# Order and counts changed in a two-layer hybrid decoder step: loads, waits and small tasks around a stream of attention units

## The chip, the core and the metric
The kernel runs on one core of a Trainium2 chip. The metric is the device time of one execution in microseconds, the median of several. The core's engines are TensorE (PE), VectorE (DVE), ScalarE (ACT), GpSimd (POOL) and SyncE (SP), whose queue here issues most of the DMA transfers.

## The reference, cut to what matters
Two layers run one after the other over 1088 rows: a prompt of 1024 tokens, and 8 requests of 8 new tokens each with 2048 cached positions. All numbers are float32.

```python
z = rmsnorm(x, norm1_g) @ w_in                 # 1024 -> 2448, feeds four mixers of 256 channels
o_a = fox attention      # 4 heads, scores + cumulative log forget gates, causal softmax
o_b = silu(layernorm(conv31(ga * sigmoid(gb)) + conv_b))            # 31 taps, per channel
o_c = g0 * compressed + g1 * selected + g2 * windowed attention     # NSA, 4 heads, one kv head
o_d = u * (tril(gmlp_ws) @ layernorm(v) + gmlp_bs)                  # chunks of 128 positions
h = x + concat(rmsnorm(o_i) * gnorm_g[i]) @ w_out
y = h + relu(rmsnorm(h, norm2_g) @ w_ff1)**2 @ w_ff2                # 1024 -> 4096 -> 1024
```
The requests' attention reads paged caches: 16 pages of 128 rows each for a request, of keys and values for fox (o_a) and of four 64-wide rows for NSA (o_c). Besides y, the new keys, values, gates and states are outputs.

## The kernel before, in words
One program per engine is written out by hand, and semaphores order them: `wait_ge(S[name], n)` holds an engine's queue until the count is there, and everything behind it in that queue waits too. A hardware loop runs the body once for each layer.

**Start of a layer.** SyncE issues the layer's small vectors ("gains"), then the token projection's weights into `Wt` in five loads (L656 to L658, counted by `w_tok`). Then come three waits (the residual stored, the normalised rows made, the first squares made) and `xt_free` is raised (L663). `xt_free` tells that the memory of the residual may be overwritten: VectorE waits for it before the taps of the convolution (L1918), GpSimd before its first two loads of raw cache pieces (L2632, two of 16 pieces). Behind it SyncE loads the mixing weights of the gMLP: `WMr` whole in one load (L664), and `WM8r`, an 8x8 corner of the four groups repeated over 8 requests by 8 blocks, in 64 loads (L665 to L668). All 65 loads count into `wm_in`, and VectorE waits for 1040 (16 a load) at L1935 before it masks both (L1937, L1938).
TensorE meanwhile forms the gate products of the convolution (L955), then tile 0 of the token projection (L1042); after that tile's second chunk it needs the masked mixing weights (`mixing_T`, L960 to L969). VectorE runs ten taps (L1911), evicts one gate product (L1923), runs twelve taps, evicts the other (L1928), forms the product with ScalarE's sigmoid, and does the masks. After that nine tiles of the token projection follow, with the other taps between.

**The stream.** Then 96 units follow: 4 heads x 8 query blocks x 3 kinds (fox, selected, windowed). In unit u TensorE forms the scores of unit u + 2, transposes the probabilities of unit u four blocks to a bank ("p" groups), multiplies those of unit u - 1 with the values, and works through the unit's extras. VectorE copies its share of the transposes, takes the row maximum of unit u + 2, and does its extras. ScalarE takes the exponentials of unit u + 1 first, then copies and extras. Every bank of transposes goes through two banks in turn (`open_group`, L1083), so TensorE waits for the copy of the group two before.
The extras are a list by unit (`extras_of`): head transposes and compressed attention, and the requests' attention, one request every ten units from unit 9. Of a request, "kt" transposes the keys of the pages (n = 0 to 7 the fox cache; n = 8 to 11 four NSA pages each; n = 12 the window), "ds" forms scores, "pt" and "pv" the values. kt 8 and 9 stand in the request's sixth unit, kt 10 and 11 in its seventh. The request's 16 NSA pages, its window and three small pieces are loaded by SyncE (`sparse_in`, L745 to L755) once "pv" of the request before is out, and count together into `sl_in`; TensorE waits for 320 per request at n = 8 (L1195).
Other steps in the stream: `gate_totals` (L2126) in unit 4, four scans of the cached gates after a wait for the stores "st0" and their copy; `lateness` (L1275) and `later_sums` (L2137) in unit 7, which make LAT; GpSimd waits for `tot_ready` and then loads the second request's cache, waits for `lat_ready` and then forms its part. `values_out` (L2211) scales the outputs of eight units, and `head_sum` (L2233) adds the three kinds of a head; both stood at the end of units 9, 17, 25, ... behind the extras (L2469 to L2472). `group_sum` (L1693) on ScalarE squares and sums finished outputs, three a unit from unit 84 on, behind the unit's extras (L1740). LAST is 88; unit 89 has "ms", unit 90 has "ee", "gc" and "hs", where "hs" on ScalarE (L1682) waits for the head's last sum from VectorE (`last_head_sum`, L2240).
After the stream the output projection and the two feed-forward products follow, each as three bf16 products (L922 and L1389), the weights streamed through two buffers.

## Time and profile before
| | |
|---|---|
| median of 3 runs | 3395.81 us (3395.05 to 3407.77) |
| the profiled execution | 3396.99 us |
| its span, first to last instruction | 3394.9 us |
| mean granted TensorE clock | 0.984 |
| PE busy | 3261.6 us, 96%, 22642 matmuls |
| DVE busy | 1455.1 us, 43% |
| ACT busy | 1009.0 us, 30% |
| POOL busy | 232.0 us, 7% |
| DMA | 312.51 MB, mean 92 GB/s |
| chain that ended last | PE 86%, DVE 4%, SPq 4%, ACT 3% |
| costliest line | L922, 10080 matmuls, 1549.1 us |

Times in the rows are microseconds from the span's start. A timeline row gives start, length, engine, line, operation, output and input, and the count of instructions merged in it; in brackets stands the idle time of the engine ahead of it, with what ended it. SPq is SyncE's queue of DMA issues; an issue is not the transfer. The granted clock is 1.00 at 2.4 GHz and 0.50 at 1.2 GHz, so a value between is a mix of the two. The first layer runs from about 20 to 1706 us, its stream from about 413 to 901.

### The profile page before, as it was taken

What the parts mean: (1) busy time and instruction counts of PE and PEld (TensorE: products, weight loads), DVE (VectorE), ACT (ScalarE), POOL (GpSimd) and SP (SyncE); (2) the same over time, 40 slices, a digit from 0 to 9 for tenths busy, and PEclk for the clock granted to TensorE, in tenths of its full rate; (3) what the DMA queues carried; (4) which work ended last, traced back from release to release, by engine and by line L of the source; (5) the groups of instructions that cost most, each with busy time, mean ns of one, the idle gap of its engine ahead of it and who ended that gap; (6) DMA issues with size and microseconds to landing.
All of it is one profiled execution on the core that took longest, in us unless ns stands there. A gap on an engine that the chain in (4) does not pass through costs nothing.

```text
span 3394.9 us, 55958 instructions
## 1 busy us (share of the span) xinstructions
PE 3261.6 (96%) x22642; PEld 1888.2 (56%) x22642; DVE 1455.1 (43%) x2795; ACT 1009.0 (30%) x1804; POOL 232.0 (7%) x172
## 2 busy tenths in 40 slices
PE   8899999998899999999999999999989999999998
PEld 5455477776644444444445555767766444444444
DVE  5965653333643311332169566433335432113312
ACT  2113344444423200321102233445453322012211
POOL 1211200000300000000002111000011000000000
PEclk9999999999999999999999999999999999999999
DMA  8423234333311210113153324334322112111322
GB/s 274 118 89 109 83 130 150 127 113 102 106 42 53 68 50 25 43 56 95 51 146 114 107 80 139 136 94 144 132 85 94 44 49 68 44 31 49 83 68 91
DMA packets 375954, 312.51 MB, mean 92 GB/s; under 512 B 121564, under 2 KB 358648, under 8 KB 368376
## 3 DMA queue, kind: packets, MB, share of 16 engines
q1 hardware_dynamic: 367912, 208.59, 21.8%
q0 software_dynamic: 7840, 101.20, 8.0%
q8 instruction: 130, 2.13, 0.3%
q14 instruction: 72, 0.59, 0.1%
HBM read 264.34 MB, written 50.46 MB: 93 GB/s over the span
## 4 chain that ended last, share of the span: by engine, by line
PE 86%; DVE 4%; SPq 4%; ACT 3%; issue 2%; DMA 1%; POOL 0%; POOLq 0%; DVEq 0%; ACTq 0%
PE PS L922 46%; PE PS L1042 13%; PE PS L1310 5%; PE PS L1333 4%; PE PS L1201 2%; PE PS L955 2%; PE PS L1359 2%; PE PS L1017 2%; PE PS L1247 1%; PE PS L1389 1%; SPq L748 1%; DVE arena L1911 1%; SPq L743 1%; PE PS L1003 1%; PE PS L1208 1%
## 5 line engine op out<-in xcount | busy, mean ns | idle before, releaser
L922 PE MATMUL PS<-arena 128*128 128x512 bf16 (+1 forms) x10080 | 1549.1, 317 | 0.0
L922 PEld LDWEIGHTS PS<-arena 128*128 128x128 bf16 x10080 | 753.4, 98 | 794.8
L1042 PE MATMUL PS<-arena 128*128 128x512 f32 (+3 forms) x1152 | 478.0, 570 | 0.0
L1494 ACT ACTIVATE arena<-arena 128x1024 bf16<-128x1024 f32 (+1 forms) x108 | 141.5, 1310 | 1089.3 <-PE PS L922 1076.0
L1042 PEld LDWEIGHTS PS<-arena 128*128 128x128 f32 (+1 forms) x1152 | 208.6, 184 | 236.8 <-issue 203.9
L2506 DVE TENSOR_TENSOR arena<-PS,arena 128x1088 f32<-128x1088 f32 (+1 forms) x48 | 62.0, 1292 | 643.1 <-PE PS L922 632.0
L1310 PE MATMUL PS<-arena 128*128 128x512 f32 (+3 forms) x576 | 232.1, 511 | 10.4 <-ACT arena L1627 5.8
L2532 DVE SCALAR_TENSOR_TENSOR arena<-PS,arena 128x1088 f32<-128x1088 f32 x64 | 82.7, 1292 | 353.1 <-PE PS L922 352.7
L1333 PE MATMUL PS<-arena 128*128 128x64 f32 x1632 | 208.2, 273 | 0.0
L1333 PEld LDWEIGHTS PS<-arena 128*128 128x128 f32 x1632 | 203.0, 196 | 0.0
L1639 ACT ACTIVATE arena<-PS 128x512 f32<-128x512 f32 x208 | 122.1, 596 | 237.2 <-PE PS L1201 236.8
L1561 ACT ACTIVATE arena<-PS,arena 128x512 f32<-128x512 f32 (+6 forms) x144 | 73.9, 581 | 357.9 <-DVEq L2050 227.1
L1911 DVE SCALAR_TENSOR_TENSOR arena<-arena 128x1024 f32<-128x1024 f32 x240 | 175.1, 781 | 2.5
L1877 DVE TENSOR_TENSOR arena<-arena 128x1024 bf16<-128x1024 f32 (+1 forms) x108 | 165.8, 1535 | 20.5 <-ACT arena L1494 20.5
L2195 DVE TENSOR_REDUCE arena<-PS 128x1 f32<-128x1024 f32 (+5 forms) x192 | 137.6, 717 | 65.1 <-PE PS L1313 64.5
L2190 DVE COPY arena<-PS 128x128 f32<-128x128 f32 (+3 forms) x136 | 68.3, 502 | 214.1 <-PE PS L1359 213.6
L1201 PE MATMUL PS<-arena 128*128 128x128 f32 x832 | 130.8, 285 | 25.5 <-DVE arena L2190 8.2
L1627 ACT ACTIVATE arena<-PS,arena 128x1024 f32<-128x1024 f32 (+5 forms) x192 | 135.6, 706 | 31.3 <-DVE arena L2195 31.2
L955 PE MATMUL PS<-arena 128*128 128x512 f32 (+1 forms) x384 | 129.4, 499 | 11.3 <-DVE arena L1886 11.3
L1359 PE MATMUL PS<-arena 128*128 128x128 f32 x816 | 130.6, 284 | 9.3 <-DVE arena L2287 2.6
L1310 PEld LDWEIGHTS PS<-arena 128*128 128x128 f32 x576 | 96.9, 200 | 61.5 <-issue 50.3
L1201 PEld LDWEIGHTS PS<-arena 128*128 128x128 f32 x832 | 96.3, 147 | 43.5 <-DVE arena L2190 10.6
(355 smaller groups left out, 2880.7 us busy)
## 6 DMA issues: line engine op xcount, KB each, us to landing
arena<-in_w_ff SPq DMA_DIRECT2D x64, 512.0 KB, 4.1
arena<-in_w_ff SPq DMA_DIRECT2D x32, 1024.0 KB, 5.7
arena<-in_cache_nsa_kv SPq DMA_DIRECT2D x256, 64.0 KB
x_s<-arena SPq DMA_DIRECT2D x24, 544.0 KB, 3.5
arena<-in_w_in SPq DMA_DIRECT2D x4, 2048.0 KB
arena<-in_w_out SPq DMA_DIRECT2D x16, 512.0 KB, 4.0
arena<-x_s SPq DMA_DIRECT2D x2, 3264.0 KB, 10.4
arena<-in_w_in SPq DMA_DIRECT2D x12, 512.0 KB, 6.7
```

The costliest lines, as they stand in the source:

```text
L922: last = mm(PS[:, 1536 * k + a:1536 * k + a + wd], ww[:, c, :], xx[:, c, a:a + wd], start=c == 0 and n == 0, stop=c == blocks - 1 and n == 2)
L955: last = mm(PS[:, 1536 * s + a:1536 * s + a + n], Wg[:, k, (2 * s + f) * P:(2 * s + f + 1) * P], XNT[:, k, a:a + n], start=k == 0, stop=k ...
L1042: last = mm(PS[0:r, c * 512:c * 512 + b - a], XNT[:, j, t * P:t * P + r], Wt[:, j, a:b], start=j == 0, stop=j == KD - 1)
L1201: last = tr(out[:, j * P:(j + 1) * P], src, ident)
L1310: last = mm(PS[:, at:at + len(part) * P], q[:, i * P:(i + 1) * P], kt[:, part[0] * P:(part[-1] + 1) * P], start=True, stop=not masks)
L1333: last = mm(PS[:, at:at + HD], PTR[u % 2][:, n * P:(n + 1) * P], v, start=n == 0, stop=n == len(js) - 1)
L1359: last = tr(out[:, (j - a) * P:(j - a + 1) * P], PR[u % 2][:, j * P:(j + 1) * P], ident)
L1494: run(WH[k][:, 0:blocks, :], src[k][:, 0:blocks, :], ACT.Copy).then_inc(S["w_hi"], 1)
L1627: run(PR[u % 2][:, 0:width], PS[:, (u % 2) * 1024:(u % 2) * 1024 + width], ACT.Exp, bias=NMX[k][:, v:v + 1], accum_out=RS[k][:, v:v + 1]). ...
L1877: V.tensor_tensor(WL[k][:, 0:blocks, :], src[k][:, 0:blocks, :], WH[k][:, 0:blocks, :], ALU.subtract)\
L1911: last = V.scalar_tensor_tensor(y, x, CWT[:, c, j:j + 1], y, ALU.mult, ALU.add)
L2195: V.reduce_max(NMX[k][:, v:v + 1], PS[:, (u % 2) * 1024:(u % 2) * 1024 + P * len(keys_of(u))], AX, negate=True).then_inc(S["nm_ready"], 1)
```

## The change
SyncE raises `xt_free` ahead of the five token weight loads, with its three waits, which so stand ahead of the loads too. `WM8r` is loaded in 32 loads, one for each request and group, each of which reads its 8x8 corner eight times over, and VectorE's count becomes 528. The pages of a request count into `sl_first` (the first eight) and `sl_in` (the rest); TensorE waits for the one at n = 8 and for the other at n = 10. `values_out` moves to the head of its unit, `head_sum` behind the row maximum of the same unit. `gate_totals` moves from unit 4 to unit 5. `lat_ready` is dropped for a second count of `tot_ready`. `group_sum` moves ahead of the extras in the units behind LAST.

```diff
@@ SyncE
-                for a, b in ((0, 512), (512, C_GLU), (C_GLU, 1156), (1156, 1424), (1424, TOKW)):
-                    src = a if a < C_GLU else a - C_GLU + C_NSA
-                    sp.dma_start(Wt[:, :, a:b], w("w_in")[:, :, src:src + b - a].rearrange("o (k p) n -> p (o k) n", p=P)).then_inc(S["w_tok"], 16)
-
                 sp.wait_ge(x_out, 128 * l + 128)
                 sp.wait_ge(S["xn_ready"], KD)
                 sp.wait_ge(S["sq_ready"], 1)
                 sp.sem_inc(S["xt_free"], 1)
+                for a, b in ((0, 512), (512, C_GLU), (C_GLU, 1156), (1156, 1424), (1424, TOKW)):
+                    src = a if a < C_GLU else a - C_GLU + C_NSA
+                    sp.dma_start(Wt[:, :, a:b], w("w_in")[:, :, src:src + b - a].rearrange("o (k p) n -> p (o k) n", p=P)).then_inc(S["w_tok"], 16)
+
                 sp.dma_start(WMr, w("gmlp_ws").rearrange("o g t s -> t (o g) s")).then_inc(S["wm_in"], 16)
                 for b in range(NB):
-                    for c in range(NB):
-                        sp.dma_start(WM8r[b * NT:(b + 1) * NT, :, c * NT:(c + 1) * NT],
-                            w("gmlp_ws")[:, :, 0:NT, 0:NT].rearrange("o g t s -> t (o g) s")).then_inc(S["wm_in"], 16)
+                    for g in range(4):
+                        sp.dma_start(WM8r[b * NT:(b + 1) * NT, g, :].rearrange("p (c s) -> p c s", c=NB),
+                            w("gmlp_ws")[:, g, 0:NT, 0:NT].rearrange("o t s -> t o s").to_broadcast([NT, NB, NT])).then_inc(S["wm_in"], 16)
@@ SyncE, sparse_in
-                                     .rearrange("o a p s d -> (o a p) s d")).then_inc(S["sl_in"], 16)
+                                     .rearrange("o a p s d -> (o a p) s d")).then_inc(S["sl_first" if j < NPG // 2 else "sl_in"], 16)
@@ TensorE, request
                         if n == 8:
-                            pe.wait_ge(S["sl_in"], 320 * (b + 1))
+                            pe.wait_ge(S["sl_first"], 16 * (NPG // 2) * (b + 1))
+                        elif n == 10:
+                            pe.wait_ge(S["sl_in"], 16 * (NPG // 2 + 4) * (b + 1))
@@ TensorE, values (GpSimd alike)
                     if u == 8:
-                        pe.wait_ge(S["lat_ready"], 1)
+                        pe.wait_ge(S["tot_ready"], 2)
@@ ScalarE, the stream
+                def group_sums(u):
+                    for x in SUMMED[SUM_EACH * (u - SUM_FROM):SUM_EACH * (u - SUM_FROM + 1)]:
+                        group_sum(x)
+
                     for a in range(0, len(keys_of(u)), 4):
                         group_out(("p", u, a))
+                    if u > LAST:
+                        group_sums(u)
                     for key in extras_of(u):
                         extra(key)
...
-                    if u >= SUM_FROM:
-                        for x in SUMMED[SUM_EACH * (u - SUM_FROM):SUM_EACH * (u - SUM_FROM + 1)]:
-                            group_sum(x)
+                    if SUM_FROM <= u <= LAST:
+                        group_sums(u)
@@ VectorE
-                dve.wait_ge(S["wm_in"], 1040)
+                dve.wait_ge(S["wm_in"], 528)
...
                 for u in range(NU):
                     h, v = u // UH_, u % UH_
+                    if u >= 2 and (u - 2) % 8 == 7:
+                        values_out((u - 2) // 8)
                     if u == 1:
                         finish(QT, 0)
                     for a in range(0, len(keys_of(u)), 4):
                         group_out(("p", u, a))
                     if u + 2 < NU:
                         row_max(u + 2)
+                    if u >= 2 and (u - 2) % UH_ == UH_ - 1:
+                        head_sum((u - 2) // UH_)
                     if u == 3:
                         gates_of_new()
-                    elif u == 4:
+                    elif u == 5:
                         gate_totals()
...
-                    if u >= 2 and (u - 2) % 8 == 7:
-                        values_out((u - 2) // 8)
-                        if (u - 2) % UH_ == UH_ - 1:
-                            head_sum((u - 2) // UH_)
```

## Rows read from the trace of the kernel before

**Rows 1.** The page's first part: busy us and share of each engine.
```profile
PE 3261.6 (96%) x22642; PEld 1888.2 (56%) x22642; DVE 1455.1 (43%) x2795; ACT 1009.0 (30%) x1804; POOL 232.0 (7%) x172
```

**Rows 2.** Timeline of TensorE, first layer's start (start us, us; idle ahead in brackets).
```profile
88.66 14.00 PE L1042 MATMUL PS<-arena 128*128 128x512 f32 x32
...
111.21 1.08 PE L964 MATMUL PS<-arena 128*128 128x128 f32 x4 [8.55 <-DVE arena L1938]
...
120.40 1.96 PE L1017 MATMUL PS<-arena 64*64 64x128 f32 x32
```

**Rows 3.** Timeline of TensorE at the second layer's start.
```profile
1778.53 13.95 PE L1042 MATMUL PS<-arena 128*128 128x512 f32 x32
...
1799.59 1.96 PE L1017 MATMUL PS<-arena 64*64 64x128 f32 x32
```

**Rows 4.** Timeline of VectorE, first layer's start.
```profile
72.06 1.21 DVE L1909 TENSOR_SCALAR arena<-arena 128x1024 f32<-128x1024 f32 x2 [9.46 <-SPq L663]
...
110.66 0.41 DVE L1938 TENSOR_TENSOR arena<-arena 64x256 f32<-64x256 f32 x1
```

**Rows 5.** Timeline of SyncE's queue (issue times), first layer's start.
```profile
58.49 13.16 SPq L658 DMA_DIRECT2D arena<-in_w_in  x5
...
79.37 25.78 SPq L667 DMA_DIRECT2D arena<-in_gmlp_ws  x64
```

**Rows 6.** Line 796's instructions: duration ns min/median/max.
```profile
L796 SPq DMA_DIRECT2D arena<-sel_s x32: 291/306/1074, 475.8 to 2159.2; - x32
```

**Rows 7.** Stretches: busy us by engine, then PEclk, DMA share, GB/s.
```profile
86.00:90.00 4.00, 4.00 (x13) 2.04 (x12) 3.96 (x6) 0.00 (x0) 0.94 (x1) 1.00 0.43 98
...
110.00:120.00 10.00, 8.79 (x32) 5.91 (x32) 9.96 (x25) 4.30 (x9) 1.08 (x1) 0.73 0.94 243
```

**Rows 8.** Timeline of TensorE, first layer's stream: five of its waits.
```profile
448.04 0.44 PE L1359 MATMUL PS<-arena 128*128 128x128 f32 x2 [2.56 <-DVE arena L2287]
...
543.63 0.66 PE L1201 MATMUL PS<-arena 128*128 128x128 f32 x4 [1.21 <-DVE arena L2190]
...
584.09 1.94 PE L1201 MATMUL PS<-arena 128*128 128x128 f32 x8 [2.73 <-DMA arena<-kvc_s]
...
783.73 0.66 PE L1201 MATMUL PS<-arena 128*128 128x128 f32 x4 [2.73 <-DVE arena L2190]
...
877.92 0.70 PE L1310 MATMUL PS<-arena 128*128 128x512 f32 x1 [2.89 <-ACT arena L1627]
```

**Rows 9.** Stretches behind waits of the stream, columns as in rows 7.
```profile
450.00:460.00 10.00, 10.00 (x53) 7.75 (x51) 5.87 (x16) 3.13 (x9) 1.15 (x1) 0.67 0.95 392
...
540.00:550.00 10.00, 8.08 (x87) 6.72 (x85) 5.31 (x21) 4.91 (x12) 0.00 (x0) 0.83 0.22 46
...
580.00:590.00 10.00, 7.27 (x37) 6.07 (x35) 3.09 (x7) 2.67 (x7) 0.00 (x0) 0.66 0.14 42
...
2130.00:2140.00 10.00, 9.44 (x82) 6.93 (x81) 8.00 (x21) 5.34 (x13) 1.15 (x1) 1.00 0.96 386
```

**Rows 10.** Timeline of SyncE's queue, third request.
```profile
560.13 20.38 SPq L748 DMA_DIRECT2D arena<-in_cache_nsa_kv  x16
...
581.54 0.62 SPq L755 DMA_DIRECT2D arena<-kvc_s  x2
```

**Rows 11.** Timeline of VectorE, unit 73.
```profile
776.34 0.29 DVE L2190 COPY arena<-PS 128x128 f32<-128x128 f32 x1 [1.82 <-PE PS L1359]
...
780.12 0.73 DVE L2219 TENSOR_SCALAR arena<-arena 128x8 f32<-128x8 f32 x1
...
781.32 0.69 DVE L2230 TENSOR_TENSOR arena<-PS,arena 128x512 f32<-128x512 f32 x1
...
782.78 0.69 DVE L2238 TENSOR_TENSOR arena<-arena 128x512 f32<-128x512 f32 x1
```

**Rows 12.** Timeline of VectorE, unit 4.
```profile
445.11 0.07 DVE L2129 MEMSET arena<- 128x15 f32 x1 [2.62 <-DMA out_gmlp_v_s<-arena]
```

**Rows 13.** Timeline of ScalarE, unit 90.
```profile
875.14 0.52 ACT L1682 ACTIVATE arena<-arena 128x384 f32<-128x384 f32 x1 [2.05 <-DVE arena L2245]
```

More of the change, by code:

```diff
@@ L444, in build_step @@
         names("raw_T raw_ev piece_next phi_in pe_in cp_T cp_ev kvc_mm kvc_ready conv_done y_mm y_ms y_rt y_ce y_sq y_no y_sg y_si y_fin z_mm z_ev z_free na_ready ex_ready lf_ready small_mm fin st0 st1 tail_T tail_ev tail_out y_out old_out")
-        names("tot_ready lat_mm lat_ready suf_ready fl_ready")
-        names("head_q head_k head_in v_in0 v_in1 gate_in kv4_in fox_ready sl_in snb_in rank_ready rank_out q_in aux_in ocb_in os_out oc_ready sm_ready ce2 dmx dex ee_ready wt_ready vb_ready s_mm nm_ready p_ready pt_T pt_evA pt_evD pv_mm o_done cs_ready ce_ready cp_ready o_ready o_out pad_ready")
+        names("tot_ready lat_mm suf_ready fl_ready")
+        names("head_q head_k head_in v_in0 v_in1 gate_in kv4_in fox_ready sl_first sl_in snb_in rank_ready rank_out q_in aux_in ocb_in os_out oc_ready sm_ready ce2 dmx dex ee_ready wt_ready vb_ready s_mm nm_ready p_ready pt_T pt_evA pt_evD pv_mm o_done cs_ready ce_ready cp_ready o_ready o_out pad_ready")
         names("od_in oh_in gn_in yb_in wo_in od_norm y_lo ss_ready h3_sq oa_hi u_hi oa_ready oa_T oa_ev y_hi")
@@ L2139, in later_sums @@
                     dve.wait_ge(S["lat_mm"], 1)
-                    V.tensor_tensor(LAT, bank(7, NH * NB).rearrange("p (h b) -> p h b", h=NH), TOT, ALU.add).then_inc(S["lat_ready"], 1)
+                    V.tensor_tensor(LAT, bank(7, NH * NB).rearrange("p (h b) -> p h b", h=NH), TOT, ALU.add).then_inc(S["tot_ready"], 1)
                 def gates_of_new():
@@ L2673, in later @@
                                     ALU.subtract).then_inc(S["suf_ready"], 1)
-                pool.wait_ge(S["lat_ready"], 1)
+                pool.wait_ge(S["tot_ready"], 2)
                 later(0)
```

## The prediction

> **What bounds the kernel now.** I read the page's engine table first. The reader is to see that TensorE is busy in 96% of the span [rows 1], so that only its idle stretches, and stretches at the lower of its two clock levels, are there to be won. The views after that follow TensorE in order of time, once through each layer, and note every idle stretch of over 1 us with what ended it. Most of it lies in two places. One is at the start of the first layer: 8.55 us before the mixing transposes (L964) [rows 2]. The second layer does the same work with no idle there [rows 3]. The others are in the stream of 96 units. Of some fifteen there in each layer, five of 1.21 to 2.89 us end with something that the change moves [rows 8]; the same five stand in the second layer, each within 0.05 us of its twin. The rest (one of 2.70 us for the group sums of unit 84 among them) end with work that it leaves in place. The long matrix products (L922) have no idle and are not touched. The third view is the granted clock in slices of 10 us: after such a wait the slice that follows often shows 0.66 to 0.83 [rows 9], which is a stretch at 1.2 instead of 2.4 GHz. The last views tell who keeps the releaser: VectorE's, SyncE's queue's and ScalarE's rows around each wait.
>
> **Taps released ahead of the token weights; mixing weights in half the loads.** The chain of the first layer's idle is this. VectorE idles 9.46 us until 72.06, released by SyncE's increment at L663 [rows 4]. SyncE is late because it first issues the five loads of L658, from 58.49 for 13.16 us [rows 5]. The taps, the gate products and the masks of the mixing weights follow on VectorE without a break to 111.07 (110.66 + 0.41), and TensorE starts L964 at 111.21 [rows 2, 4]. After the change the increment falls at about 58.5; the three waits ahead of it are long met (in the second layer too, where the increment is late for nobody, since VectorE comes to the taps later). VectorE then starts the taps at 62.6 (72.06 - 9.46), where its own work lets it, and the whole chain is 9.46 us earlier: masks done at 101.6, before TensorE has finished L1042 at 102.66 (88.66 + 14.00). The idle goes. What is late next is TensorE itself. The price includes the clock: slice 110 to 120 has 0.73 [rows 7]. Measured from the start of L1042 to the start of L1017, the first layer takes 120.40 - 88.66 = 31.74 us, the second 1799.59 - 1778.53 = 21.06 [rows 2, 3]. I take the difference, **10.7 us**, once.
>
> Two things could cut it. The masks wait for the mixing weights. SyncE issues 64 small loads (L667) from 79.37 in 25.78 us, 0.40 us each [rows 5]; 32 loads of twice as many runs remain. A load of the new kind, 64 runs of eight numbers, is L796's: median 0.306 us, and 0.29 to 1.07 over its 32 [rows 6]. So 32 of them take about 11 us and are out at 91, ten before VectorE asks. If an issue costs by its runs, it is 0.80 each, they are out at 105, and landing as the page's small loads do in some 2 us gives masks at 108.1: the gain is 3.1 instead of 10.7. I take the former, since L796's row has the same shape. Moving the increment also lets GpSimd start its two loads of cache pieces (1 MB each, L2628) some 13 us earlier, among the token weights, which L971 waits for. The bytes are the same and the DMA engines stop being full in slice 86 to 90 (share 0.43) [rows 7]; even if the token weights were last of all they would be there by 87.7, and TensorE comes at 88.66. Cost 0, at worst 1.3.
> The Trainium skill, page "DMA: Bandwidth & Descriptors", section "Queues, rings and completion order", says that an engine takes packets from its queues in turn, so the two cache pieces would take their share and the token weights land later than now. By that rule this part loses up to 1.3 us; by the row nothing.
>
> **Gate totals one unit on.** At unit 4 VectorE idles 2.62 us for a store (the "st0" count) until 445.11, then does the four scans [rows 12]; TensorE waits 2.56 us at 448.04 for the "cd" copy that stands behind them [rows 8]. One unit later the same wait still ends at 445.11, as nothing moves the store. Only the row maximum and a small copy leave the queue ahead of "cd". So I take 0.6 us a layer, **1.2**; bounds 0 and 2 x 2.56. The merged counter (tot_ready 2 for lat_ready) and the later start of the second cache load cost nothing: that load is wanted ten units on.
>
> **Pages in two counts.** The third request's first page transpose waits 2.73 us for a DMA at 584.09 [rows 8]. SyncE issues its 16 pages from 560.13 in 20.38 us and the last small load ends at 582.16 [rows 10]. The first eight, all that n = 8 and 9 read, are issued by 570.3, eleven us before TensorE asks at 581.36. The other count is asked for one unit later at n = 10; by then the last load has had some 2 us to land after 582.16, and a unit of TensorE's own work, over 3 us, lies behind 581.36, so it is met. Gain 2.73 a layer, **5.5**. The other requests have no wait of over 1 us here.
>
> **Outputs of eight units at a unit's head.** VectorE's block of values_out, with the head's sums, runs from 780.12 to 783.47 at the end of unit 73, and the copy that TensorE waits for stands behind it; TensorE idles 2.73 us at 783.73 [rows 8, 11]. At the head of the unit the same values are ready (they are of two units before), and VectorE has 1.82 us of idle ahead of its copy at 776.34 [rows 11]; values_out without the odd first row is some 1.3 us, so it fits. The sums (2 x 0.69) go behind the row maximum of 776.55, where VectorE waits for TensorE anyway. Gain 2.73 a layer, **5.5**. The same block costs 1.21 at 543.63, **2.4** for two layers [rows 8]. What is late next there is ScalarE's evacuation, within some tenths. At the eight other places of a layer the block was and stays hidden by the score products ahead of the next transposes: taken as 0, bounds -1.2 (it moves off) and +1.9 (780.12 to 782.01, in the way of a copy) each.
>
> **Gate sums ahead of the extras.** ScalarE idles 2.05 us for the head sum at 875.14, then runs three group sums, and only then the exponentials that TensorE waits 2.89 us for at 877.92 [rows 8, 13]. The sums now fall into that wait, and the head sum itself comes earlier, as values_out has left its front. ScalarE then waits for nothing but the row maximum. I step its queue through with the same durations and get 876.0 for 877.92: 1.9 a layer, **3.8**; bounds 1.4 (the sums alone) and 2.89.
>
> **The clock behind the waits.** Slices behind the waits at 543.63 and 584.09 show 0.83 and 0.66, so 1.7 and 3.4 us are lost [rows 9]; behind 783.73 I take as much as behind 584.09. That is 8.5 a layer, 17 in all, if it returns in full. It does not: at full speed other short waits for the evacuating engines come out that the slow clock hides. I take 0.6 of it, **10.2**; bounds 0 and 17, and 3.3 more if the slice at 450 to 460 (0.67) is won too [rows 9].
> The Trainium skill, page "TensorE: Matmul & The Clock Gate", Part 1, calls the slow stretch run-variable: where the gate's phase falls decides how much of one kernel is slow. By that rule the term is anything from 0 to 17. This trace agrees: the wait at 448.04 was followed by 0.67, its twin in the second layer by 1.00 [rows 8, 9].
>
> **The sum.** 10.7 + 1.2 + 5.5 + 2.4 + 5.5 + 3.8 = 29.1, and 10.2 of clock: 39.3 us. The profiled execution took 3396.99, 2.1 over its span of 3394.9, and 1.2 over the median of 3395.81. So 3396.99 - 39.3 = 3357.7 by the profile, and 3356.5 by the median; I say 3357.
>
> **Rivals.**
> The clock stays as it is: the slow stretches come elsewhere, and 29.1 is all: 3368. For it speaks the twin at 2130 to 2140, against it that four of the five waits have a slow slice behind them.
> The mixing loads cost by their runs: 3396.99 - (39.3 - 7.6) = 3365. L796's row speaks against it.
> The waits of the stream only change their name: VectorE and ScalarE are each used again within a microsecond, and another evacuation takes the place of each. Then the first layer's 10.7 alone is left: 3386. For it speaks that many short waits for ScalarE's copies stand in both layers too; against it, that these five are each ended by one named block that leaves.
> Slower: values_out at the head stands in the way of the unit's own copy and row maximum at the eight places a layer that were hidden. Each costs 1.24 us of block and 2.0 of clock, 3.24 x 16 = 52, and the 11.7 + clock of the reordered part is not won; 21.5 of the rest stays: 3427. It decides from 1.35 us a place. Against it: values two units old are ready before that copy is asked for, and VectorE idles ahead of it in rows 11.
>
> **Chances.** Forecast 0.53, clock stays 0.22, loads by runs 0.07, names change 0.13, slower 0.05. The range goes from full clock with all bounds (3396.99 - 29.1 - 20.3 - 2, about 3345) to clock and loads both missed (3375.5), with some us for what is unmeasured: 3342 to 3380. What can be told from no change is about 0.5%, 17 us, so 3379 to 3413 is "same": faster 0.82, same 0.13, slower 0.05.
>
> **What would show it.** L1909 at about 62.6 and no idle before L964; the last issue of L667 near 91; no wait for a DMA at the pages' transposes; no wait for L2190 behind L2238; L1703 ahead of L1682 in unit 90 and the wait before the score product there about 1 us; the wait at unit 5 still near 2 us. A masks' wait that ends with the mixing loads, or as much idle in the stream as now, would make it wrong.

## The result, and the profile after

| kernel | median of the runs | lowest to highest | profiled execution: time, span |
|---|---|---|---|
| before | 3400.94 us (4 runs) | 3395.05 to 3407.77 | 3396.99, 3394.9 |
| changed | 3360.84 us (4 runs) | 3354.07 to 3364.99 | 3360.78, 3358.7 |

The ratio is 0.9879, 95% interval 0.9851 to 0.9908: 40 us faster. A second series gave 0.9869 (0.9848 to 0.9891). The forecast was 3357 us, in a range of 3342 to 3380, so the time lies 4 us from it. The sum started from a profiled execution of 3396.99 us and took off 39.3 us; the gain itself was measured as 40 and 42 us. The two profiled spans differ by 36.2 us.

The page of the changed kernel, engine table. Against [rows 1], TensorE is busy for 22.8 us less, though its work is the same. Only about half of that is clock: 198 matmul records are missing from this trace, all of them of L922, whose busy time is 10.7 us lower for it (1538.4 for 1549.1). In a second profile of the changed kernel, with all 22642 records, TensorE is busy for 3248.0 us, 13.6 less than before. Records are missing in several of the traces below too.

```profile
PE 3238.8 (96%) x22444; PEld 1878.6 (56%) x22642; DVE 1451.6 (43%) x2795; ACT 1008.1 (30%) x1804; POOL 231.1 (7%) x172
```

The start of the first layer, TensorE in order of time, answering to [rows 2] (start, duration, instruction, idle time before it and who ended it).

```profile
87.95 14.00 PE L1042 MATMUL PS<-arena 128*128 128x512 f32 x32 [0.26 <-DMA arena<-in_w_in]
...
101.79 0.60 PE L964 MATMUL PS<-arena 128*128 128x128 f32 x4
...
109.06 1.96 PE L1017 MATMUL PS<-arena 64*64 64x128 f32 x32
```

The idle time of 8.55 us before L964 is gone. From L1042 to L1017 it now takes 109.06 - 87.95 = 21.11 us for 31.74, and the second layer's 21.06 [rows 3]. The 0.26 us at the front is new: the token weights land last now. VectorE and SyncE's queue show why, answering to [rows 4, 5].

```profile
61.64 1.03 DVE L1916 TENSOR_SCALAR arena<-arena 128x1024 f32<-128x1024 f32 x2
...
99.46 0.68 DVE L1944 TENSOR_TENSOR arena<-arena 128x512 f32<-128x512 f32 x1
100.06 0.41 DVE L1945 TENSOR_TENSOR arena<-arena 64x256 f32<-64x256 f32 x1
```

```profile
58.03 17.75 SPq L662 DMA_DIRECT2D arena<-in_w_in  x5
75.97 3.38 SPq L664 DMA_DIRECT2D arena<-in_gmlp_ws  x1
79.44 15.85 SPq L667 DMA_DIRECT2D arena<-in_gmlp_ws  x32
```

The taps start at 61.64, 10.42 us sooner, and the masks (L1944, L1945) have no wait. The five weight loads take 17.75 us to issue where they took 13.16, and the 32 mixing loads 15.85 us, one every 0.495 us.

The stream, TensorE, answering to [rows 8]. The first line is a wait that is new, at the first transposes of the first layer's stream; the second a wait near unit 26 that [rows 8] does not have; the third what is left of the wait before the score product of unit 90; the fourth the wait at unit 5 in the second layer.

```profile
400.87 3.61 PE L1092 MATMUL PS<-arena 128*66 128x128 f32 x16 [2.61 <-DMA arena<-qa_s]
...
529.44 2.63 PE L1112 MATMUL PS<-arena 128*128 128x32 f32 x16 [1.20 <-ACT arena L1620]
...
840.71 1.98 PE L1312 MATMUL PS<-arena 128*128 128x512 f32 x4 [0.79 <-ACT arena L1629]
...
2095.51 0.44 PE L1361 MATMUL PS<-arena 128*128 128x128 f32 x2 [3.12 <-DVE arena L2294]
```

Of the five waits of [rows 8], those of 1.21, 2.73 (pages) and 2.73 us (unit 73) are gone, the 2.89 us of the score product is 0.79, and the 2.56 us of the gate totals is 0.44 in the first layer, but 3.12 in the second. The new wait of 2.61 us is for the load of the first head's queries (`qa_s`). The kernel before waits 1.21 us for VectorE there. Slices of 10 us with a clock under full are fewer, but they are there, also in places where [rows 9] has none:

```profile
400.00:410.00 10.00, 7.56 (x37) 4.74 (x37) 7.76 (x15) 4.39 (x8) 6.28 (x4) 0.83 0.96 267
...
530.00:540.00 10.00, 10.00 (x62) 7.72 (x65) 2.31 (x5) 3.65 (x9) 0.00 (x0) 0.66 0.00 0
...
850.00:860.00 10.00, 7.31 (x29) 3.87 (x28) 7.09 (x12) 3.34 (x7) 3.14 (x2) 0.74 0.07 16
```

**How the gain divides.** Each run lists its span and its mean granted clock. Their product varies less than the span within one kernel (24 runs of the kernel before: standard deviation 2.2 us for 4.5, and span and clock correlate at -0.88). The rest of the span is what the low clock took. (The mean clock of a run is on record with three digits, so a single product is good to 1.7 us.) Means over the runs:

| kernel | runs | ratio to before (95%) | span | span x clock | rest |
|---|---|---|---|---|---|
| before, three series | 24, 9, 23 | 1 | 3401.0, 3398.6, 3398.9 | 3339.7, 3340.4, 3340.8 | 61.2, 58.2, 58.1 |
| changed | 4 | 0.9879 (0.9851 to 0.9908) | 3358.1 | 3320.4 | 37.8 |
| changed, again | 5 | 0.9869 (0.9848 to 0.9891) | 3355.5 | 3321.9 | 33.6 |

Against the first two series of the kernel before, 19 us of about 43 are in the product and 23 to 25 in the clock. (An idle microsecond in a slow stretch counts half in each, so the product shows less than the idle time that went.)

### The profile page after: what moved, and what is told of

It is laid out like the page before. It is cut to its first block, busy times and chain, and to the rows that moved or that the text cites. A ratio compares the mean times of both kernels' runs of the same rounds, so it can differ in the third digit from the quotient of the medians.

```text
span 3358.7 us, 55654 instructions
## 1 busy us (share of the span) xinstructions
PE 3238.8 (96%) x22444; PEld 1878.6 (56%) x22642; DVE 1451.6 (43%) x2795; ACT 1008.1 (30%) x1804; POOL 231.1 (7%) x172
## 4 chain that ended last, share of the span: by engine, by line
PE 89%; ACT 3%; DVE 3%; SPq 2%; issue 2%; DMA 1%; POOL 0%; POOLq 0%; ACTq 0%; DVEq 0%
PE PS L922 46%; PE PS L1042 14%; PE PS L1312 5%; PE PS L1335 4%; PE PS L1203 3%; PE PS L955 2%; PE PS L1361 2%; PE PS L1017 2%; PE PS L1249 1%; PE PS L1391 1%; PE PS L1210 1%; PE PS L1003 1%; PE PS L1215 1%; PE PS L1031 1%; PE PS L1092 1%
## 5 line engine op out<-in xcount | busy, mean ns | idle before, releaser
L922 PE MATMUL PS<-arena 128*128 128x512 bf16 (+1 forms) x9882 | 1538.4, 316 | 10.4
L922 PEld LDWEIGHTS PS<-arena 128*128 128x128 bf16 x10080 | 753.4, 98 | 794.8
L1042 PE MATMUL PS<-arena 128*128 128x512 f32 (+3 forms) x1152 | 477.6, 570 | 0.3 <-DMA arena<-in_w_in 0.3
L1042 PEld LDWEIGHTS PS<-arena 128*128 128x128 f32 (+1 forms) x1152 | 208.3, 184 | 237.0 <-issue 203.6
L1335 PEld LDWEIGHTS PS<-arena 128*128 128x128 f32 x1632 | 202.4, 196 | 0.0
L1312 PEld LDWEIGHTS PS<-arena 128*128 128x128 f32 x576 | 95.1, 196 | 55.8 <-issue 48.8
L2544 DVE TENSOR_TENSOR arena<-arena 128x1088 f32 (+1 forms) x64 | 82.6, 1291 | 86.9 <-ACT arena L1792 86.9
```

The lines of the kernel that those rows point to most:

```text
L922: last = mm(PS[:, 1536 * k + a:1536 * k + a + wd], ww[:, c, :], xx[:, c, a:a + wd], start=c == 0 and n == 0, stop=c == blocks - 1 and n == 2)
L1042: last = mm(PS[0:r, c * 512:c * 512 + b - a], XNT[:, j, t * P:t * P + r], Wt[:, j, a:b], start=j == 0, stop=j == KD - 1)
L1312: last = mm(PS[:, at:at + len(part) * P], q[:, i * P:(i + 1) * P], kt[:, part[0] * P:(part[-1] + 1) * P], start=True, stop=not masks)
L1335: last = mm(PS[:, at:at + HD], PTR[u % 2][:, n * P:(n + 1) * P], v, start=n == 0, stop=n == len(js) - 1)
```

## The experiments

### Parts of the change, put into the kernel before

**Part A alone** (taps and mixing loads, the two hunks of the load section and the count 528):

```
+ (xt_free and its waits)
  for a, b in (...): dma Wt[:, :, a:b]
- (xt_free and its waits)
- 64 loads of WM8r, wm_in 1040
+ 32 loads of WM8r, wm_in 528
```

> The kernel before with part A alone: the tap sums released ahead of the token weights, and the mixing weights in 32 loads. Theory (the step of the forecast): the first layer's start shortens by the idle time in front of the mixing products, TensorE from its first token product to the product behind the mixing transposes 21.1 us instead of 31.7, and nothing else moves: -10.6 us, ratio about 0.997. Rival (loads cost by their runs): VectorE waits for the loads behind its taps, that stretch stays over 26 us and the gain is under 6 us.

Measured: 3386.53 us (7 runs), to 3403.59 for the kernel before in the same series, ratio 0.9961 (0.9942 to 0.9980); product 3333.0, rest 51.8. The profile, TensorE, from the first token product to the product behind the mixing transposes, and two of its waits in the stream, at the first transposes and for the gate totals:

```profile
89.97 14.00 PE L1042 MATMUL PS<-arena 128*128 128x512 f32 x32 [0.96 <-DMA arena<-in_w_in]
...
111.08 1.97 PE L1017 MATMUL PS<-arena 64*64 64x128 f32 x32
...
402.60 3.50 PE L1092 MATMUL PS<-arena 128*66 128x128 f32 x16 [2.32 <-DMA arena<-qa_s]
...
435.74 0.44 PE L1359 MATMUL PS<-arena 128*128 128x128 f32 x2 [0.90 <-DVE arena L2287]
```

The stretch is 21.11 us, as in the changed kernel. The theory holds for this stretch. The wait for the token weights is 0.96 us here, but it is 0.91 in the kernel with parts D and E only, so it is not shown to be a cost of this edit.

Its "nothing else moves" does not hold. TensorE comes to the stream some 10 us sooner. In six of the eight profiles of kernels that hold part A whole it then waits 2.1 to 2.6 us for `qa_s`, in none of the six without it. On the other side the waits in the stream that hang on a DMA are shorter with it: the one for the gate totals, in unit 4, is 0.90, 1.28, 1.77 and 1.90 us with part A (this kernel and one below) and 2.22 to 3.57 us in twelve places without, and the one for the pages 1.65 and 1.64 us for 2.71 to 2.77 in the kernel before. Why these loads land sooner is not shown; SyncE, which issues them, has 32 loads fewer in each layer. By the ratio the kernel gains 13 us, by the mean spans 16, both more than 10.6: 6.7 us stand in the product and 9.4 in the clock (51.8 for 61.2).

**The taps alone, with the 64 loads kept:**

> The kernel before with the tap sums released early, but the 64 small loads of the mixing weights kept. Theory: both edits are needed. VectorE starts its taps at 61.6 us and is done near 99.5, but the 64 loads are issued only by 79.4 + 64 x 0.40 = 105 us and land about 2 us later, so VectorE idles some 8 us for them and only 2 to 4 us of the 10.6 are left. Rival (the loads were never in the way, the taps' release is all of it): the stretch from the first token product to the one behind the mixing transposes is 21 to 22 us, as with both.

Measured: 3396.62 us (12 runs), ratio 0.9978 (0.9967 to 0.9989); product 3338.6. VectorE, SyncE's queue and TensorE:

```profile
109.00 0.69 DVE L1937 TENSOR_TENSOR arena<-arena 128x512 f32<-128x512 f32 x1 [7.07 <-DMA arena<-in_gmlp_ws]
```

```profile
81.33 26.57 SPq L667 DMA_DIRECT2D arena<-in_gmlp_ws  x64
```

```profile
110.17 1.09 PE L964 MATMUL PS<-arena 128*128 128x128 f32 x4 [6.30 <-DVE arena L1938]
```

VectorE is early, and waits 7.07 us for the loads; TensorE waits 6.30 us instead of 8.55 (7.00 in the second profile of the kernel before), and its stretch is 30.67 us for 31.74 and 31.14. So 0.5 to 2.3 us are the taps' alone, at or under the 2 to 4 expected, and the rest needs fewer loads as well. The 32 loads of the changed kernel end at 95.29 and VectorE asks at 99.46: they are 4 us ahead and not ten, and the landing comes off that.

**Part C alone** (pages in two counts; `lat_ready` merged into `tot_ready`, gate totals left in unit 4):

```
- .then_inc(S["sl_in"], 16)
+ .then_inc(S["sl_first" if j < NPG // 2 else "sl_in"], 16)
- pe.wait_ge(S["sl_in"], 320 * (b + 1))
+ pe.wait_ge(S["sl_first"], ...) at n == 8, pe.wait_ge(S["sl_in"], ...) at n == 10
```

> The kernel before with part C alone: the pages counted in two semaphores (and the two gate counts merged into one, with the gate totals left where they were). Theory: the wait of 2.73 us at the pages' transposes of the first request goes in each layer, 5.5 us, and with it the granted clock of the ten microseconds behind it returns to full, up to 3 us a layer: -8.5 to -11.5 us, ratio 0.9966 to 0.9975. Rival 1 (only the idle time comes back, the slow stretch moves elsewhere): -5.5 us. Rival 2 (the wait takes another name at the second half of the pages, two units on): nothing.

Measured: 3395.64 us (12 runs), ratio 0.9976 (0.9964 to 0.9989), -8 us; product 3336.4, rest 56.3. At the pages' transposes there is no wait:

```profile
582.60 1.28 PE L1203 MATMUL PS<-arena 128*128 128x128 f32 x8
```

One unit on, where the second count is asked for, there is none over 0.42 us either, so the wait took no other name. The kernels that keep the one count show 1.60 to 2.78 us there: it ends with a DMA, and its size is not the same in each execution. The time cannot tell the theory (8.5 to 11.5 us) from its first rival (5.5 us): the interval holds both, with 3.3 us in the product and 4.9 in the clock.

**Parts D and E alone** (outputs of eight units at the head, head sum behind the row maximum):

```
  for u in range(NU):
+     if u >= 2 and (u - 2) % 8 == 7: values_out((u - 2) // 8)
      ...  row_max(u + 2)
+     if u >= 2 and (u - 2) % UH_ == UH_ - 1: head_sum(...)
-     (both at the end of the unit)
```

> The kernel before with parts D and E alone: the outputs of eight units at the head of a unit on VectorE, the head's sum behind the row maximum. Theory: the waits of 1.2 us at unit 25 (two, one a layer) and 2.7 us at unit 73 (two) go: -7.9 us, and the granted clock behind them makes it -5 to -12. Rival 1 (the wait takes another name: the softmax of the unit or its p copies run late instead): under 3 us. Rival 2 (the outputs stand in the way of the p copy at each eighth unit): slower, 1 us at each of 22 places.

Measured: 3380.32 us (6 runs), ratio 0.9935 (0.9916 to 0.9954), -22 us; product 3334.5 (-5), rest 44.5 (-17). Near unit 25 and at the score product of unit 90:

```profile
545.77 2.23 PE L1112 MATMUL PS<-arena 128*128 128x32 f32 x16 [1.20 <-ACT arena L1618]
...
865.87 1.98 PE L1310 MATMUL PS<-arena 128*128 128x512 f32 x4 [1.38 <-ACT arena L1627]
```

Both targeted waits are gone. The second line shows something that the forecast put down to another part: the 2.89 us before the score product are already 1.38, since the last outputs leave VectorE sooner. The waits removed come to 2 x (1.20 + 2.72 + 1.51) = 10.9 us. Not all of that is won: all of TensorE's idle time in the two streams is 91.2 us, for 94.7 and 97.0 in the two profiles of the kernel before, so it fell by some 5 us, as the product did. Waits of under 0.9 us each come to 41.3 us for 35.3 to 37.8. The gain of 22 us, nearly twice what was expected at the most (12), is for the greater part clock. The forecast's slower rival has no support: against the kernel with the taps alone, no row maximum of the stream loses over 0.8 us at the eight places a layer, and what one loses the next gives back.

**Part F alone** (the group sums of units 89 to 92 ahead of the extras):

```
+ if u > LAST: group_sums(u)
  for key in extras_of(u): extra(key)
- if u >= SUM_FROM: ...
+ if SUM_FROM <= u <= LAST: group_sums(u)
```

> The kernel before with ScalarE's group sums of the last four units ahead of the extras, nothing else. Theory (the reading of the values-only kernel, in which the wait at unit 90's score product fell from 2.89 to 1.38 us): the order alone takes the sums' 1.4 us out of the way behind the head sum, 2.89 becomes 1.5 in both layers, -2.8 us in all, too little for the timed runs to tell from noise (ratio 0.998 to 1.000). Rival (the forecast's step holds as one piece and needs both edits: ScalarE waits for the head's sum anyway): 2.89 stays.

Measured: 3396.94 us (12 runs), ratio 0.9987 (0.9974 to 1.0000).

```profile
874.22 1.98 PE L1310 MATMUL PS<-arena 128*128 128x512 f32 x4 [1.77 <-ACT arena L1627]
```

2.89 became 1.77 in both layers: the order alone gives 1.1 us, not 1.4. With both edits 0.79 is left.

The ratios of A, C, D with E, and F alone multiply to 0.986, the whole measured 0.987 and 0.988: within their intervals the parts add up.

**The kernel before, again:**

> The kernel before once more, unaltered, for a second profile. In the first one TensorE has no wait for ScalarE's p copy (L1618) at the products of unit 26, where a wait of 1.20 us stands in every kernel run since, also in those that leave part D out. Theory: that wait belongs to the kernel before too, and the first profile lacks it because its clock was low there (540 to 550 us at 0.83), so that the copy came in time; part D's price is read against the second profile. Idle waits of 1.2, 2.9 and 8.5 us at units 25 and 89 and ahead of the mixing products return within 0.1 us, those that end with a DMA within 1 us. Rival: the 1.20 us is made by the new instruction order and is absent here again.

Measured: 3397.75 us (12 runs) to 3401.25, ratio 0.9984 (0.9972 to 0.9996), span of the profile 3406.6. The same program against itself comes out 0.16% faster, with an interval that leaves 1 out: the series tell no difference under about 0.2%. F alone is one such, and the taps alone (0.22%) and part C (0.24%) are barely clear of it; what is said of these three rests on their profiles.

```profile
543.34 0.66 PE L1201 MATMUL PS<-arena 128*128 128x128 f32 x4 [1.20 <-DVE arena L2190]
...
548.07 1.97 PE L1112 MATMUL PS<-arena 128*128 128x32 f32 x16 [1.20 <-ACT arena L1618]
```

The wait of 1.20 us for ScalarE's copy near unit 26 is the kernel's own. [rows 8] lacks it where the clock was low (0.83 from 540 to 550 us, 1.00 in this second profile), so that the copy was in time. The second layers of both profiles lack it too, with 0.83 and 0.81 from 2220 to 2230 us; the other twelve profiles have it in both layers. In the stream, waits that instructions set are back within 0.05 us. Of those that hang on a DMA, the one for the gate totals is 3.54 and 2.22 us (2.56 and 2.51 in the first profile) and the one for the group sums' load 2.90 and 4.47 (2.70 and 1.73 in the first profile). The one ahead of L964, which hangs on SyncE's issues, is 7.00 for 8.55.

### The gate totals (part B), in the changed kernel

**The changed kernel, again:**

> The changed kernel once more, unaltered, for a second profile and a firmer ratio beside the next three. Theory: the waits of TensorE that instructions decide come back to within 0.1 us, and what differs between two profiles of one program is where slices of 10 us show a clock under 1.00 (their sum 41 us in the first profile) and how long the queue takes for the stores ahead of the gate totals. Ratio 0.985 to 0.991. Rival: waits elsewhere in the stream move by more than 0.5 us too, and then no single wait can be read from one profile.

Measured: 3357.92 us (5 runs), ratio 0.9869. The wait for the gate totals is neither 0.44 nor 3.12 now:

```profile
438.11 0.66 PE L1361 MATMUL PS<-arena 128*128 128x128 f32 x2 [1.82 <-DVE arena L2294]
...
817.74 0.66 PE L1225 MATMUL PS<-arena 128*32 128x128 f32 x8 [2.72 <-ACT arena L1620]
...
2104.55 0.44 PE L1361 MATMUL PS<-arena 128*128 128x128 f32 x2 [2.35 <-DVE arena L2294]
```

The second line was 1.56 us in the first profile; it ends with the group sums' load. The wait of 2.61 us for `qa_s` is not there either; 1.21 us for VectorE stands in its place. So the rival is right for waits with a DMA behind them, and the theory for all others.

**Gate totals back in unit 4** (`elif u == 5` to `elif u == 4`):

> The changed kernel with part B undone: the gate totals back in unit 4. Theory: VectorE asks one unit earlier for stores that land when they did, so the wait of 0.44 us in the first layer and of 3.12 us in the second grows by 1 to 2 us each, and the kernel is 2 to 5 us slower than the changed one. Rival (unit 5 was the worse place in the second layer, where the wait grew from 2.51 to 3.12 us): the same time or less than the changed kernel.

Measured: 3365.65 us (5 runs), ratio 0.9900 (0.9885 to 0.9915); product 3321.8, rest 42.4.

```profile
435.40 0.44 PE L1361 MATMUL PS<-arena 128*128 128x128 f32 x2 [1.77 <-DVE arena L2294]
...
2097.19 0.69 PE L1361 MATMUL PS<-arena 128*128 128x128 f32 x2 [1.90 <-DVE arena L2294]
```

The theory failed in the profile: 1.77 and 1.90 in unit 4 against 0.44 to 3.12 (mean 1.93) in unit 5, and the product of span and clock is the changed kernel's to 0.1 us. The two kernels of the next section that leave the totals in unit 5 show 1.83, 0.44, 0.43 and 0.44 us, 0.44 being what is left when the stores have landed. So the mean is 1.4 us over eight places in unit 5, and 1.5 us over the four in unit 4 with part A. The median is 8 us higher, all of it clock, with intervals that still touch. Whether that is the edit's is open.

**Gate totals in unit 6**, the sums over later requests (both engines) in unit 8:

> The changed kernel with the gate totals in unit 6 and the sums over later requests (both engines' parts) in unit 8. Theory: the stores have landed by then, the waits of 0.44 and 3.12 us are gone, the clock of 2090 to 2110 us is full in the profile: 3.6 us less from idle time and up to 7 with the clock. Rival: the gate sums of the first request come a unit later from GpSimd, and TensorE waits for them or VectorE's sum at unit 8 delays the row maximum: no gain or a new wait of 1 to 3 us between units 8 and 14.

Measured: 3356.74 us (4 runs), ratio 0.9872 (0.9852 to 0.9891); product 3322.6.

```profile
442.44 0.31 PE L1172 MATMUL PS<-arena 128*32 128x64 f32 x4 [0.96 <-DVE arena L2197]
```

The wait for the stores is gone in both layers, but a new one of 0.96 us stands at the compressed outputs behind it, in both. All of TensorE's idle time in the two streams is 78.5 us, for 78.8 and 80.7 in the profiles of the changed kernel, and the time is the same. The rival's second half was near the truth.

### The group sums in the changed kernel

**All sums ahead of the extras.** (SUM_FROM is unit 84, so the units are 84 to 92 here and 85 to 93 below: the expectations count them one too high.)

```
- if u > LAST: group_sums(u)
+ if u >= SUM_FROM: group_sums(u)
```

> The changed kernel with ScalarE's group sums behind the p copies and ahead of the extras in all of units 85 to 93, not only in the last four. In the changed kernel ScalarE goes from three sums (1.5 us) straight into the exponentials and the p copy, and TensorE waits 1.56, 1.34 and 1.64 us for that copy in units 85 to 88. Theory: the sums then fall into ScalarE's idle time before the copies of the request (0.9, 1.1, 1.2 us) and the three waits shrink by 1 us or more each: -3 to -4 us a layer, -6 to -10 in all with the clock. Rival: the request's transposed copies (L1641) come 1.5 us late instead and TensorE waits at its products for them: no change; slower if the sums of unit 85 wait longer for their load.

Measured: 3359.39 us (4 runs), ratio 0.9879 (0.9862 to 0.9896); product 3318.8. TensorE and, below, ScalarE:

```profile
814.98 1.30 PE L1361 MATMUL PS<-arena 128*128 128x128 f32 x5 [3.87 <-ACT arena L1641]
...
832.68 0.33 PE L1238 MATMUL PS<-arena 128*128 128x128 f32 x1 [1.27 <-ACT arena L1643]
```

```profile
812.05 0.42 ACT L1705 ACTIVATE arena<-arena 128x256 f32<-128x256 f32 x1 [4.21 <-DMA arena<-o_s]
```

The waits of 1.64 us went and 1.34 became 1.27, as the theory has it; but the first sum is now asked for before its load has landed, and TensorE waits 3.87 us for the request's copy behind it (4.34 in the second layer). It came to nothing, as the rival had it.

**The same, one unit later:**

```
- SUM_FROM, SUM_EACH = LAST - 4, 3
+ SUM_FROM, SUM_EACH = LAST - 3, 3
```

> The changed kernel with the group sums ahead of the extras in all their units and begun one unit later (units 86 to 94). The run before it had them ahead of the extras from unit 85: the waits of 1.64 us went, but at unit 85 ScalarE met sums whose load had not landed and TensorE waited 3.9 and 4.3 us. Theory: one unit on, the load is there: that wait goes too, and against the changed kernel (2.7, 1.3, 1.6 us in units 85 to 88 of its second profile) 4 us a layer are gained, 8 us in all and up to 12 with the clock: ratio about 0.9845. Rival: 25 sums in nine units end one unit later, the last group norms of units 93 and 94 wait for them, and it is even.

Measured: 3348.90 us (5 runs) to 3401.25, ratio 0.9848 (0.9827 to 0.9869); product 3316.7, rest 31.5. No wait of TensorE behind that load is left. But one of 2.29 us at unit 89 is new, and it is not of the kind that was expected. TensorE, then VectorE, then GpSimd:

```profile
842.16 0.28 PE L1267 MATMUL PS<-arena 128*24 128x128 f32 x1 [2.29 <-DVE arena L2195]
```

```profile
837.49 2.28 DVE L2224 TENSOR_SCALAR arena<-arena 128x8 f32<-128x8 f32 x1
```

```profile
835.20 4.54 POOL L2702 TENSOR_TENSOR arena<-arena 128x2048 f32<-128x2048 f32 x1
```

L2224 has 8 numbers a partition and takes 0.17 us in the median of its 24 places. Here it takes 2.28, and ends at 839.77, 0.03 us after GpSimd's product of 2048 a partition ends at 839.74. GpSimd starts its norm on the ninth sum. With the sums a unit later the norm falls on the outputs of unit 89. In the changed kernel GpSimd's product ends at 832.50, before VectorE comes to them. VectorE's two instructions ahead of L2224, a sum and a copy (L2366 and L2367), start during the same GpSimd product and take 0.60 and 0.28 us, as they do elsewhere: not every instruction is held.

The kernel before has the same thing in a smaller form. The row of [rows 11] at 780.12 (L2219) takes 0.73 us and ends at 780.85, 0.03 us after this one of GpSimd:

```profile
779.67 1.15 POOL L2671 TENSOR_TENSOR arena<-arena 128x512 f32<-128x512 f32 x1 [21.23 <-PE PS L1219]
```

The Trainium skill, page "SBUF — State Buffer", section "Who interferes with whom", says that VectorE in some modes and GpSimd share a port pair as an exclusive lock, so that the later one blocks fully. This trace agrees: VectorE's instruction is held to the end of GpSimd's, 0.03 us behind it in both kernels.

**Both:** this and the gate totals in unit 6.

> The changed kernel with the gate totals in unit 6 (the sums over later requests in unit 8) and the group sums ahead of the extras from unit 86 on: both of the edits that the runs point to. Theory: they add up. The gate totals gave about 1 us of idle time a layer net of the new 0.96 us at unit 6's copy, the group sums 4: 10 us off the changed kernel, 3348 us, ratio 0.984. Rival (clock: what idle time saves, slow stretches elsewhere take back): as the changed kernel, 0.987 to 0.988.

Measured: 3348.87 us (5 runs), ratio 0.9848 (0.9829 to 0.9868); product 3315.3, rest 32.1. That is the time of the kernel with the late sums alone. Both beat the changed kernel's 3360.84 and 3357.92 by 9 to 12 us. The intervals still overlap by 0.002, but the products lie 4 to 7 us below its 3320.4 and 3321.9, where the mean of five runs scatters by 0.8 to 1.4.

## Why the prediction was right

**Taps and mixing weights (10.7).** 31.74 became 21.11: 10.6 (31.14 in the second profile of before, so 10.0 against that). The mechanism and the size are as forecast. Two of its numbers were off and cost nothing. The mixing loads follow each other every 0.495 us and not every 0.345, where the 64 before did every 0.40. The median of one is 0.278 us in both kernels (the row that was read, of another line, has 0.306), but a few take up to 1.99 us, and the mean is 0.40 for 0.30. And the token weights do land last, at 87.90, against the 87.7 that the bound gave. The wait of 0.26 us is inside the bound of 1.3, and so is the 1.22 us of the changed kernel's second profile. The rule that the prediction took from the Trainium skill, page "DMA: Bandwidth & Descriptors", section "Queues, rings and completion order" (an engine takes packets from its queues in turn), is not told apart from another cause: the loads' issue also grew, from 13.16 to 17.75 us. What the step left out is what it does to the stream: the new wait for `qa_s`, and the shorter waits for other loads.

**Gate totals (1.2).** Worth nothing by the rows: 1.4 us in unit 5 and 1.5 in unit 4, with part A in both. The wait did get shorter than in the kernel before (2.8 us over twelve places), but already with part A alone. The step fails at "the same wait still ends at 445.11, as nothing moves the store". The store does move. It is the last of a dozen behind SyncE's load L722, whose issue took 0.94 to 10.58 us in the profiles. The last of them leaves SyncE 21.7 us behind the stream's first row maximum in the first layer of the changed kernel, and 24.7 in the second: that spread is more than one unit on can give. "Still near 2 us" holds for two of the changed kernel's four values (1.82, 2.35) and not for 0.44 and 3.12.

**Pages (5.5).** The wait is gone in both layers and took no other name: right. Its size in the kernel before is 2.71 to 2.77 us in both profiles, but 1.60 to 2.78 over all kernels with one count, and 1.65 with part A alone. So 5.5 is the upper end, and beside part A it may be worth only 3.3.

**Outputs at the head (2.4 and 5.5).** Right for the named waits: 1.20 and 2.72 us a layer, and no single wait of weight at the other places, though the short ones grew. Of the 2.72, 0.56 us was VectorE's L2219, held by GpSimd; the prediction saw its odd length and left it unexplained. What is "late next" at unit 25 is a wait of 1.20 us for ScalarE and not some tenths; it was there before, hidden by slow stretches in the one profile read.

**Group sums (3.8).** 2.89 - 0.79 = 2.1 a layer, 4.2: right in size, but the cause is divided otherwise. The outputs' move gives 1.5 of it by itself, the order 1.1 by itself, both 2.1.

**The clock (10.2).** The one term that was much too small. By the rows, the waits removed are 8.3 + 5.5 + 2.4 + 5.4 + 4.2 = 25.8 us, and the total of TensorE's idle time in the two streams fell by less than the last four (17.5), since others vary: from 94.7 and 97.0 us in the two profiles of before to 78.8 and 80.7, so by 16, which with the 8.3 makes 24. That leaves 42 - 24 = 18 for the clock, of which 10.6 - 8.3 = 2.3 stand in the first term. So 16 against 10.2, within the bounds of 0 and 20.3. The factor of 0.6 was chosen by argument; the full sum of the slices (17) would have been nearer. By the clock column of the runs it is 23 to 25 us, with those 2.3 among them: by that reading the term lies at the upper bound or past it.

29.1 without the clock was thus some 3 us too much (24 + 2.3 = 26.3; part B, and idle time that came back as other waits) and the clock some 6 too little. The two errors have opposite signs, and 3 us are left of them: that the sum came so near is in part luck, and the range of 38 us was wide enough for either error alone. **The rivals:** "the clock stays" is out by the clock column; "loads by runs" by 0.495 us an issue, as 0.80 would have put the last at 105; "the waits only change their name" by part C and by the time of D/E alone, though in D/E some 6 of the 10.9 us did come back as other waits; "slower" by D/E alone.

## What to carry to other kernels

In this kernel, whose matrix engine is 96% busy, 24 us of idle time went together with 18 us or more of low clock. So price a wait of 1 to 3 us in such a stream at its own length and nearly as much again. Read that price from many runs, as span times granted clock and the rest, since one profile shows slow stretches at places that change from run to run, and they hide other waits. A wait that ends with a DMA needs several profiles before its length may stand in a sum. When a block of work is moved to another time, look also at what the engines that wait for it will then start. When the start of a stage comes sooner, look at whether its first loads do too.

## What the runs showed of the hardware that was not expected

- Spans of one kernel vary by 20 us (3389.8 to 3410.4 in 24 runs of the kernel before), while the product of span and mean granted clock has a standard deviation of 1.1 to 3.4 us in every kernel: most of the scatter of these runs is TensorE's clock.
- A slice at a clock of 0.66, in which TensorE was busy throughout, follows a wait of only 1.20 us (530 to 540 us of the changed kernel, behind 529.44); the slice before it has 1.00.
- A VectorE instruction of 0.17 us took 2.28 us (`tensor_scalar`, 128x8) and ended 0.03 us after a GpSimd product; one of the same kind took 0.73 us in the kernel before and ended 0.03 us after a GpSimd product too. It shows as the length of a tiny instruction and not as a wait.
- One queue issue of the same load (L722) takes 0.94 to 10.58 us, in the same place of the same or nearly the same program.
